# First unit of three products multiplied from un-normed h, inside the fill of the normed operand

## The reference, cut to what matters

```python
def rms_norm(x, g):
    x32 = x.astype(jnp.float32)
    y = x32 * lax.rsqrt(jnp.mean(x32 * x32, axis=-1, keepdims=True) + EPS)
    return (y * g.astype(jnp.float32)).astype(x.dtype)
...
h = h + dsa_attention(rms_norm(h, g_attn_a[layer]), w_in_a[layer], w_o_a[layer])
h = h + sq_relu_mlp(rms_norm(h, g_mlp[layer]), w_up[layer], w_down[layer])
...
k, v, f_logit = jnp.split(rms_norm(h, g_kv) @ w_kv, [B_QK, 2 * B_QK], axis=-1)
```

## Time and profile before

| | us |
|---|---|
| median of three runs | 2683.11 |
| the profiled execution, its own time | 2682.6 |
| its span in the profile | 2681.3 |
| PE busy | 2619.2 (98%) |
| DVE busy | 1269.1 (47%) |
| POOL busy | 1252.6 (47%) |
| ACT busy | 979.0 (37%) |

### The profile page before, as it was taken

How to read it: one execution, slowest core, us unless ns; L and a number is a source line. 1 busy time by engine, 2 the same in 40 slices (tenths; PEclk the granted TensorE clock), 3 DMA queues, 4 the chain that set the end, 5 groups by cost and what they waited for, 6 DMA issues and landing times.

```text
span 2681.3 us, 32087 instructions
## 1 busy us (share of the span) xinstructions
PE 2619.2 (98%) x12938; PEld 2107.6 (79%) x12938; DVE 1269.1 (47%) x2103; ACT 979.0 (37%) x1620; POOL 1252.6 (47%) x618
## 2 busy tenths in 40 slices
PE   8989999999999999999999999999999999999999
PEld 5757888888776888888766788888788888888887
DVE  4863798842035398882556341221336233431121
ACT  4464433223347332232457342332324223342231
POOL 4865444444456444444467444444344343444442
PEclk9999999999999999999999999999999999999999
DMA  4201555532220265542210232332432222233222
GB/s 144 63 17 48 173 186 182 188 110 80 94 79 1 84 209 185 182 163 96 80 48 2 63 95 95 96 97 90 146 98 79 94 95 79 80 109 95 94 94 79
DMA packets 259431, 274.41 MB, mean 102 GB/s; under 512 B 6868, under 2 KB 249300, under 8 KB 259028
## 3 DMA queue, kind: packets, MB, share of 16 engines
q1 hardware_dynamic: 259284, 272.37, 31.4%
HBM read 270.26 MB, written 2.10 MB: 102 GB/s over the span
## 4 chain that ended last, share of the span: by engine, by line
PE 93%; DVE 2%; ACT 2%; POOL 1%; issue 1%; DMA 0%; SPq 0%; DVEq 0%
PE bank L448 24%; PE bank L450 24%; PE bank L449 24%; PE bank L604 2%; PE bank L580 2%; PE bank L617 2%; PE bank L516 2%; PE bank L518 2%; PE bank L517 2%; PE bank L424 2%; PE bank L425 2%; PE bank L428 1%; PE bank L568 1%; PE bank L844 1%; PE bank L716 1%
## 5 line engine op out<-in xcount | busy, mean ns | idle before, releaser
L1697 POOL TENSOR_TENSOR wlo<-raw,whi 128x1024 fp32r<-128x1024 f32 (+1 forms) x408 | 984.6, 2434 | 1202.1 <-ACT whi L893 1201.9
L448 PE MATMUL bank<-Xhi,whi 128*128 128x512 f32 (+1 forms) x1616 | 641.0, 397 | 1.5 <-POOL wlo L1697 1.5
L450 PE MATMUL bank<-Xhi,wlo 128*128 128x512 f32 (+1 forms) x1616 | 630.6, 390 | 0.0
L449 PE MATMUL bank<-Xlo,whi 128*128 128x512 f32 (+1 forms) x1616 | 629.9, 390 | 0.0
L893 ACT ACTIVATE whi<-raw 128x1024 fp32r<-128x1024 f32 (+1 forms) x408 | 404.9, 1041 | 571.8 <-PE bank L450 497.4
L448 PE MATMUL bank<-Hhi,whi 128*128 128x512 f32 x1024 | 401.0, 392 | 0.0
L450 PE MATMUL bank<-Hhi,wlo 128*128 128x512 f32 x1024 | 399.4, 390 | 0.0
L449 PE MATMUL bank<-Hlo,whi 128*128 128x512 f32 x1024 | 398.9, 390 | 0.0
L448 PEld LDWEIGHTS bank<-Xhi,whi 128*128 128x128 f32 (+1 forms) x1616 | 302.6, 187 | 72.0 <-issue 8.1
L449 PEld LDWEIGHTS bank<-Xlo,whi 128*128 128x128 f32 (+1 forms) x1616 | 302.7, 187 | 65.0 <-issue 3.2
L450 PEld LDWEIGHTS bank<-Xhi,wlo 128*128 128x128 f32 (+1 forms) x1616 | 302.4, 187 | 65.1
(11 more groups left out here) (268 smaller groups left out, 3160.4 us busy)
## 6 DMA issues: line engine op xcount, KB each, us to landing
ada<-in_ada_w SPq DMA_DIRECT2D x48, 1024.0 KB, 5.5
raw<-in_w_up SPq DMA_DIRECT2D x32, 1024.0 KB, 5.4
raw<-in_w_down SPq DMA_DIRECT2D x32, 1024.0 KB, 4.9
raw<-in_mlp_w_in SPq DMA_DIRECT2D x32, 1024.0 KB, 5.4
raw<-in_mlp_w_out SPq DMA_DIRECT2D x32, 1024.0 KB, 4.9
raw<-in_gmlp_w_in SPq DMA_DIRECT2D x24, 1024.0 KB, 5.1
raw<-in_gmlp_w_out SPq DMA_DIRECT2D x12, 1024.0 KB, 5.0
raw<-in_w_in_a SPq DMA_DIRECT2D x8, 1024.0 KB, 5.3
```

What stands on the lines that cost most here:

```text
L448: pe.matmul(b[0:rows, :], whi[s][:, c, j:j + rows], hi[:, c, :], start=(c == 0), stop=False)
L449: pe.matmul(b[0:rows, :], whi[s][:, c, j:j + rows], lo[:, c, :], start=False, stop=False)
L450: m = pe.matmul(b[0:rows, :], wlo[s][:, c, j:j + rows], hi[:, c, :], start=False, stop=(c == KC - 1))
L1697: pool.tensor_tensor(wlo[u % 2][:, c0:c1, 0:k], src[:, c0:c1, 0:k], whi[u % 2][:, c0:c1, 0:k].bitcast(F32), ALU.subtract).then_inc(lo_done, 1)
```

## The change

`PLAIN` names the three operands. Per chunk, after h is complete, ACT writes a high part of `HT * gain` and DVE the low part (`plain`), into halves of the `Hhi`/`Hlo` buffers that are free then. `fm` gets a further leading unit: unit 0 is multiplied from these chunks with no factor in them, and the mean matmuls and the row matmuls are placed inside it, before chunks 2 and 4. Unit 1 is then the unit multiplied as the fill delivers. In the `WHOLE` events the last chunk is not halved any more, and its squares are added to the sum. ACT and POOL split unit 1 before the fill, not behind it (`ahead=1`). ACT copies the rows from bank 6 to `rstd` for all three (`keep_rows`), and the fill takes its factors from `rstd`. In the fill, after the sixth chunk's product, DVE multiplies tiles 0 and 1 by `rstd` into `held` (`scale_tile`); ACT evacuates them from `held` after the whole fill is over (`unscaled`).

```diff
+PLAIN = ("m0", "kv", "m1")
+WHOLE = ("oa", "m0", "ob")
@@ tensor_program
-        def fm(name, source, chunk, after=None, first=None):
+        def fm(name, source, chunk, after=None, first=None, plain=None):
-            if first:
-                s = gm.unit % 2
+            leads = [(source, first, chunk)] if first else []
+            if plain:
+                at = KC * PLAIN.index(plain)
+                leads.insert(0, (PLAIN_AT[plain], lambda c: pe_until.wait_ge(plain_hi, at + c + 1), lambda c: pe_until.wait_ge(plain_lo, at + c + 1)))
+            for i, ((hi, lo), high, whole) in enumerate(leads):
...
                 for c in range(KC):
                     if c % 4 == 0:
+                        wait_unit_half(u, c // 4)
+                    if plain and i == 0 and c == 2:
+                        mean_squares(EVENT_OF[plain])
+                    if plain and i == 0 and c == 4:
+                        norm_rows(EVENT_OF[plain])
+                    high(c)
...
-            for i in range(int(first is not None), len(gm.widths)):
+            for i in range(len(leads), len(gm.widths)):
...
-        norm_rows("oa")
...
-        norm_rows("m0")
-        fm("kb", X, lambda c: wait_chunk("kv", c), first=lambda c: wait_high("kv", c))
+        fm("kb", X, lambda c: wait_chunk("kv", c), first=lambda c: wait_high("kv", c), plain="kv")
...
-        norm_rows("ob")
@@ scalar_program
+        def plain(f, gain, g, c):
+            act_until.wait_ge(*freed(g))
+            if f == "kv" and c == 0:
+                act_until.wait_ge(tile_done, GEMM["m0d2"].end)
+            act.activation(PLAIN_AT[f][0][:, c, :], HT[:, c, :], ACT_F.Copy, scale=gain[:, c:c + 1]).then_inc(plain_hi, 1)
+        def keep_rows(f):
+            act_until.wait_ge(rows_full, 2 * EVENTS.index(EVENT_OF[f]) + 3)
+            act.activation(rstd[:], bank[6][:], ACT_F.Copy).then_inc(rows_kept, 1)
+        def unscaled(f, g, o):
+            if f in PLAIN and o < 2:
+                by_dve, by_pool = low_parts(f, KC - 1)
+                act_until.wait_ge(x_lo, by_dve)
+                act_until.wait_ge(x_lop, by_pool)
+                act_until.wait_ge(scaled, 2 * PLAIN.index(f) + o + 1)
+                return held[o]
+            wait_tile(g)
+            return bank[g % 4]
...
         root("oa")
+        split(GEMM["m0u0"].unit + 1)
+        keep_rows("m0")
         fill("m0", None, GEMM["oa"].end)
...
-        units("kb", keep_heads("kb", KB))
+        units("kb", keep_heads("kb", KB), ahead=1)
@@ vector_program, fill
+                if c == 0 and f in PLAIN:
+                    dve_until.wait_ge(rows_kept, PLAIN.index(f) + 1)
                 dve.scalar_tensor_tensor(tmp[c % 4][:], HT[:, c, :], gain[:, c:c + 1], rows[:], ALU.mult, ALU.mult).then_inc(xq_done, 1)
+                if c == 5 and f in PLAIN:
+                    for o in range(2):
+                        scale_tile(f, GEMM["kb" if f == "kv" else f + "u0"].tile + o, o)
...
+        def plain(f, gain, c):
+            hi, lo = PLAIN_AT[f]
+            dve_until.wait_ge(plain_hi, KC * PLAIN.index(f) + c + 1)
+            dve_until.wait_ge(h_set, h_at[c])
+            dve.scalar_tensor_tensor(lo[:, c, :], HT[:, c, :], gain[:, c:c + 1], hi[:, c, :].bitcast(F32), ALU.mult, ALU.subtract).then_inc(plain_lo, 1)
+        def scale_tile(f, g, o):
+            wait_tile(g)
+            dve.tensor_tensor(held[o][:], bank[g % 4][:], rstd[:], ALU.mult).then_inc(scaled, 1)
...
         for o in range(KC):
-            add_to_h(GEMM["oa"].tile + o, o, halves=(o == KC - 1))
+            add_to_h(GEMM["oa"].tile + o, o)
             add_square("oa", o)
+            if o < KC - 1:
+                plain("m0", VEC["g_mlp0"], o)
         recip("oa")
+        plain("m0", VEC["g_mlp0"], KC - 1)
         wait_rows("oa")
-        fill("m0", VEC["g_mlp0"], None, bank[6])
+        fill("m0", VEC["g_mlp0"], None, rstd)
```

More of the change, by code:

```diff
@@ L88, in square_base @@
 def square_base(e):
[L89 to L97, removed]
+    done = added = halves = 0
+    for x in EVENTS[:EVENTS.index(e)]:
+        sums = 2 if x == "m1" else 1
+        done += KC * sums
+        added += (KC - 1 if x in WHOLE else KC - 2) * sums
+        halves += 0 if x in WHOLE else sums
+    return done, added, halves
 class Until:
@@ L416, in fm @@
                 for j in range(2):
-                    wait_bank(gm.tile + j)
+                    wait_bank(g + j)
                 for c in range(KC):
                     if c % 4 == 0:
-                        wait_unit_half(gm.unit, c // 4)
-                    first(c)
+                        wait_unit_half(u, c // 4)
[3 more added lines that the diff above has]
+                        norm_rows(EVENT_OF[plain])
@@ L422, in fm @@
+                    high(c)
                     for j in range(2):
-                        b = bank[(gm.tile + j) % 4]
+                        b = bank[(g + j) % 4]
                         pe.matmul(b[:], whi[s][:, c, j * P:(j + 1) * P], hi[:, c, :], start=(c == 0), stop=False)
                         pe.matmul(b[:], wlo[s][:, c, j * P:(j + 1) * P], hi[:, c, :], start=False, stop=False)
-                    chunk(c)
+                    whole(c)
                     for j in range(2):
-                        m = pe.matmul(bank[(gm.tile + j) % 4][:], whi[s][:, c, j * P:(j + 1) * P], lo[:, c, :], start=False, stop=(c == KC - 1))
+                        m = pe.matmul(bank[(g + j) % 4][:], whi[s][:, c, j * P:(j + 1) * P], lo[:, c, :], start=False, stop=(c == KC - 1))
@@ L531, in to_rows, with mean_squares @@
             m.then_inc(done, 1)
[L533 to L537, removed]
+        def mean_squares(e, gain=False):
+            done, added, halves = square_base(e)
+            both, whole = 1 + gain, e in WHOLE
+            pe_until.wait_ge(sq_add, added + (KC - 1 if whole else KC - 2) * both)
             for k, total in enumerate((rstd, gained)[:both]):
                 for i in range(NT):
-                    pe.matmul(bank[6 + i // 2][:, 2 * k + i % 2:2 * k + i % 2 + 1], total[:, i * P:(i + 1) * P], mean[:],
-                              start=(k == 0 and i % 2 == 0), stop=False, skip_group_check=True)
+                    m = pe.matmul(bank[6 + i // 2][:, 2 * k + i % 2:2 * k + i % 2 + 1], total[:, i * P:(i + 1) * P], mean[:],
+                                  start=(k == 0 and i % 2 == 0), stop=(whole and i % 2 == 1), skip_group_check=True)
+                    if whole and i % 2:
+                        m.then_inc(ms_full, 1)
+            if whole:
+                return
             for h in range(2):
@@ L725, in mlp @@
                 if f == "u":
-                    fm(name, X, lambda c: wait_chunk(f"m{m}", c), done, first=(lambda c: wait_high(f"m{m}", c)) if g == 0 else None)
+                    fm(name, X, lambda c: wait_chunk(f"m{m}", c), done, first=(lambda c: wait_high(f"m{m}", c)) if g == 0 else None,
+                       plain=f"m{m}" if g == 0 and m < 2 else None)
                 else:
@@ L919, in square @@
         def square(e, g, c, gain=None):
-            done, added = square_base(e)
+            _, added, halves = square_base(e)
             both = 1 if gain is None else 2
+            split_last = c == KC - 1 and e not in WHOLE
             if c == KC - 2:
                 act.activation(warm[:], eps[:, 0:1], ACT_F.Sqrt)
[L925 to L928, removed]
+            for h in range(1 + split_last):
+                at = slice(256 * h, 256 * h + 256) if split_last else slice(0, S)
+                if split_last and h == 0:
+                    act_until.wait_ge(half_set, EVENTS.index(e) - len(WHOLE) + 1)
                 else:
@@ L999, in up @@
                         act_until.wait_ge(h_hi, v - 1)
-                    act.activation(tmp[v % 2][:], bank[(gm.tile + o) % 4][:], ACT_F.Relu).then_inc(up_q, 1)
+                    act.activation(tmp[v % 2][:], src[:], ACT_F.Relu).then_inc(up_q, 1)
                     act_until.wait_ge(up_q, v + 1)
@@ L1010, in down @@
                         square(f"m{m}", gm.tile + o, o, GS if m == 1 else None)
-                units(f"m{m}{f}{g}", up if f == "u" else down)
+                        if m == 0:
+                            plain("kv", VEC["g_kv"], gm.tile + o, o)
+                units(f"m{m}{f}{g}", up if f == "u" else down, ahead=int(m < 2 and stage == 0))
         for i in range(NT):
@@ L1118, in scalar_program, with evac_ob @@
         attend("b")
-        units("ob", lambda o: square("ob", GEMM["ob"].tile + o, o))
+        def evac_ob(o):
+            square("ob", GEMM["ob"].tile + o, o)
+            plain("m1", VEC["g_mlp1"], GEMM["ob"].tile + o, o)
+        units("ob", evac_ob)
         root("ob")
+        split(GEMM["m1u0"].unit + 1)
+        keep_rows("m1")
         fill("m1", None, GEMM["ob"].end)
@@ L1545, in vector_program @@
         for o in range(KC):
-            add_to_h(GEMM["ob"].tile + o, o, halves=(o == KC - 1))
+            add_to_h(GEMM["ob"].tile + o, o)
```

(13 more changed lines are left out.)

63 lines of the change are left out of this document (40 added, 23 removed).

## The result

| kernel | median us | runs | ratio to before, 95% interval |
|---|---|---|---|
| before | 2682.66 (2680.08 to 2683.48) | 13 | |
| changed | 2688.26 (2684.99 to 2693.62) | 13 | 1.0024 (1.0017 to 1.0032) |

The forecast was 2684.2 in 2673 to 2689, with 0.60 on "same". The median lies inside the range, but the change is clearly slower, where I forecast a difference that can't be told from none: the medians are 5.6 us apart, and the interval of the ratio is 4.6 to 8.6 us. The profiled execution took 2690.46 us, its span is 2689.2, 7.9 over the span before: it is one of the slower runs.

A forecast was written before the change was run, and what follows sets the result against it. PE, busy 2619.2 of 2681.3 us, was taken as the bound. Savings of 4.1 us up to the third units and 5.2 us of slow clock gave +1.1: own time 2683.7, median 2684.2, range 2673 to 2689.

The forecast's parts named there:

- same: Whole kernel: a time that can't be told from no change, within about 0.2% (5.4 us); chance 0.60.
- What stays at the norm itself: PE at each of three norms: only 2.11 us of the 6.75 or 7.5 is left, with no pause.
- The fill late and slower: DVE's fill: starts at 8.2 us after the un-normed unit's start, is held up by POOL, over at 22.3.
- The third unit's split: Split behind evacuations after the fill: PE waits 4.2 us in m0 and m1, 2.9 in kb; 4.1 saved in all.
- The clock behind the waits: PE after the third units' waits: slow clock costs 2.1 us each in m0 and m1, 1.0 in kb, together 5.2.
- The step that failed: First ada block on DVE in m0 and m1: starts some 4 us later, costs at most 0.5 us, taken as 0.
- Rival D: Between fill's end and third unit's split, DVE and POOL hold each other up more: +8.8 us, 2692; chance 0.12.
- Rival C: No wait at the third unit, fill from rstd as fast as from a bank, no clock fall: 2668; chance 0.12.

The follow-up runs named there:

- Kernel 7: Changed kernel with the third unit's split ahead of the evacuations, fill factors from bank 6 and the whole ada schedule four tiles later: 2666.75 us, ratio 0.9941.
- Experiment 3: Changed kernel with the three fills taking their factors from bank 6 instead of rstd, the copy into rstd kept: 2682.80 us, ratio 1.0000.
- Experiments 1: Changed kernel with ACT's split of the third unit ahead of the evacuations of tiles 0 and 1: 2687.77 us, ratio 1.0021.
- kernel 6: Changed kernel with the third unit's split ahead of the evacuations and the whole ada schedule four tiles later, factors still from rstd: 2668.42 us, ratio 0.9948.
- experiment 2: Changed kernel with the ada sums on PE and their outputs on DVE two tiles later, the blocks staying: 2685.34 us, ratio 1.0010.
- kernel 5's: Changed kernel with the whole ada schedule (loads, blocks, sums, outputs) four tiles later: 2685.18 us, ratio 1.0012.
- 9: Changed kernel with fill factors from bank 6 and the ada schedule four tiles later, the split still behind the evacuations: 2671.08 us, ratio 0.9957.

## Why the prediction was wrong

- **What stays at the norm itself: right.** No wait at the mean or row matmuls, no idle. From T the second unit's matmuls are issued after 23.6 us, where 23.88 was forecast: 1.9 us a norm instead of 2.1. Kernel 7 shows it by itself. In its profile the three norms are 16.2 us shorter than before, for the 15.5 forecast; the whole is 14.6 below the before beside it (14.0 in the profiles), the rest being lost at falls of the clock elsewhere. That its 2666.75 meets the prediction's 2667 to 0.3 us is partly luck.
- **The fill late and slower: right.** Over at T + 21.7 against 22.3. Experiment 3 shows the cause. By the Trainium skill (SBUF — State Buffer, Who interferes with whom) a DVE instruction with two SBUF inputs contends with a GpSimd instruction that reads SBUF, over a pair of ports that is an exclusive lock; the trace agrees, 2.77 us against 1.40 for the same two products.
- **The third unit's split: right.** Starts at T + 27.8, 26.5, 28.0 against 28.1, 26.8, 28.1. Experiments 1 and 6, where the split is moved, take the wait down to 0.5.
- **The clock behind the waits: right in kind, short in size.** 5.2 us charged; 6.1 measured behind the three third units (1.5, 1.7, 2.9), and 1.4 more behind the wait that I had not got. The time up to the third units was 4.8 us less than before, for 4.1 forecast. So all that the sum had comes to +1.3 in the profile, for +1.1.
- **The step that failed** is the sentence on the `ada` block: "PE asks for that block's sum after tile 4, when it is just done, and that is at most 0.5 us; I take 0." "Just done" only comes out if the block, moved 4 us, keeps its length of 8.2 us, though the prediction's own paragraph on the fill rests on DVE and POOL holding each other up. What moves the block also puts the fourth unit's split right behind the third's, so that the block stands under four halves of POOL instead of two: 12.2 us. PE waited 2.6 and 0.8 us, and the clock fell once more. In the profile that is 5.5 us, by experiment 2 it is 3.8. With it the forecast's +1.1 becomes 4.9 to 6.6, against 5.6 between the medians and 6.8 in the profile's three stretches.
- Rival D had the sign and the place, DVE and POOL behind the fill, but another mechanism. Its sign was a fill that ends after T + 23; it ended at T + 21.7. The scalings cost next to nothing: from the third product to POOL's last `Xlo` the fill took 10.14 us with them, `qb`'s fill 10.13 without. The squares and low parts of tiles 0 and 1 took 0.69 each. Rival C's time, 2668, at 0.12, is about what the change is worth once the split and the `ada` schedule are in other places: 2668.42 in kernel 6, 2666.75 in 7.

## What to carry to other kernels

A block of work that a change delays must be timed anew at its new place, against what runs beside it there; its old duration belongs to its old neighbours. When work is pulled ahead of a fill, look for what is still queued behind the fill on each engine (here the next weights' split behind two evacuations): that is where the saved time goes, and on PE the two pauses of 4 us cost another 1.5 and 2.9 us behind them. And when one such order is mended and the time stays, look whether the next engine in the line has any pause left; here each mend alone gave 0.0 to 0.2% less than the changed kernel, and together with the later schedule 0.8%.

## What the runs showed of the hardware that I had not expected

- While POOL runs instructions back to back, DVE gets one instruction through for each of them, ending 0.1 to 0.3 us behind it: 2.50 us each for a 128x256 instruction with two inputs in SBUF that takes 0.50 alone. It was so in `m0` and `m1` of the changed kernel and in experiment 3. The block's first instruction, which has only one tensor as input, stood as well when POOL's half started with it: 2.53 us in `m0`, 0.35 in `m1`, where it started first. POOL's four halves took 9.79 us in `m0` and 10.1 in experiment 3, where in `kb`, with DVE idle, they took 9.37: POOL pays 0.1 to 0.2 us for each.
- Behind waits of 1.9 to 2.7 us the clock can fall or hold at the same place: 2.7 us fell in the profiles of the changed kernel and of experiment 2 and held in kernel 5's; 1.92 fell in `m0` and held in `m1` of experiment 3; 1.76 held twice in 9. All six waits of 4.0 to 4.2 fell. A fall cost 1.4 to 2.9 us in the changed kernel's profile.
- Such falls also come far from the change, in some profiles and not in others: in attention B the clock fell in eight of the eleven other kernels' profiles and not in that of before. The 13 runs of the changed kernel spread over 8.6 us, the 13 of before over 3.4, but 33 others of before over 7.7; so the spread is no sign of the change by itself.
